# A gated hybrid decoder layer on eight cores: weights packed block by block, and the first projection of the head fed tile by tile

## The reference, cut to what matters

```
h    = rmsnorm(x, g_mix)
proj = h @ w_in                              # 1024 -> 3584: a | u | v | gate_a | gate_b
z    = gelu(proj[u, v])
v    = rmsnorm(z[v], g_v)                    # per row, over 512
s    = causal 128x128 mix of v inside each chunk of 128 rows (w_s, b_s)
pa   = (windowed means of a, windows 2,4,8,16, minus a) @ w_pool * s_pool
x    = x + (gate_a * (pa @ w_pool_out) + gate_b * ((u*s) @ w_gmlp_out)) @ w_out
h2   = rmsnorm(x, g_ffn)
x    = x + (silu(h2 @ w_gate) * (h2 @ w_up)) @ w_down
y    = rmsnorm(x, g_final)
```

## Time and profile before

| | us |
|---|---|
| median of 3 runs (872.39 to 930.36) | 873.85 |
| profiled execution, its own time | 876.13 |
| span of its slowest core, core 5 | 874.6 |
| spans of cores 0, 2, 3, 7 | 873.6, 867.3, 872.8, 873.3 |

### The profile page before, as it was taken

One profiled execution on the slowest core, in us unless ns is written; L12 is line 12 of the kernel. 1 busy time (PEld: TensorE's weight loads), 2 busy tenths in 40 slices (PEclk: granted clock), 3 DMA queues, 4 the chain that ended last, 5 costly groups with the idle time before them and its releaser, 6 DMA issues.

```text
span 874.6 us, 13055 instructions; the slowest of 8 cores (867.3 to 874.6 us)
## 1 busy us (share of the span) xinstructions
PE 824.1 (94%) x4584; PEld 437.0 (50%) x4584; DVE 370.3 (42%) x609; ACT 248.4 (28%) x452; POOL 142.3 (16%) x174
## 2 busy tenths in 40 slices
PE   0599999999999999999997999999999999999996
PEld 0346666655666666644443454444544444444442
DVE  1458644456322222244566593344722112114446
ACT  3654522224321121120146452222531111110012
POOL 2320011021201110000235211101120101000003
PEclk9989999999999999999998899999999999999998
DMA  8896346574966573544378942667587566356304
GB/s 205 191 139 87 73 56 86 75 103 69 113 81 81 65 93 43 84 70 75 54 209 233 110 56 28 80 85 98 68 99 95 65 81 85 50 84 88 57 16 177
DMA packets 102482, 81.05 MB, mean 93 GB/s; under 512 B 5324, under 2 KB 96964, under 8 KB 102403
## 3 DMA queue, kind: packets, MB, share of 16 engines
q0 software_dynamic: 94048, 58.10, 50.7%
q1 hardware_dynamic: 7390, 20.88, 7.5%
q10 hardware_dynamic: 981, 1.24, 0.7%
HBM read 129.76 MB, written 9.01 MB: 159 GB/s over the span
## 4 chain that ended last, share of the span: by engine, by line
PE 89%; DMA 5%; DVE 2%; issue 1%; ACT 1%; POOL 1%; SPq 1%; DVEq 0%; POOLq 0%; ACTq 0%
PE ps L346 87%; DMA xbuf<-xp 2%; DMA ring<-w_in 2%; PE ps L396 1%; DVE hb L384 1%; SPq L304 1%; POOL rs L364 0%; PE ps L647 0%; ACT hT L404 0%; PE ps L600 0%; DVE ps L653 0%; DVEq L926 0%; ACT junk L355 0%; DVE ovl L658 0%; DVE shr L538 0%
## 5 line engine op out<-in xcount | busy, mean ns | idle before, releaser
L346 PE MATMUL ps<-hT,ring 128*128 128x384 bf16 (+2 forms) x2720 | 489.9, 340 | 2.5 <-ACT hT L404 1.3
L346 PEld LDWEIGHTS ps<-hT,ring 128*128 128x128 bf16 x2720 | 266.2, 98 | 211.3 <-issue 11.4
L346 PE MATMUL ps<-ring,ovl 128*128 128x512 bf16 (+1 forms) x1020 | 224.3, 379 | 0.0
L748 DVE TENSOR_TENSOR ovl<-ftmp,ps 128x384 bf16<-128x384 f32 (+2 forms) x110 | 64.2, 585 | 241.0 <-PE ps L346 238.1
L346 PEld LDWEIGHTS ps<-ring,ovl 128*128 128x128 bf16 (+1 forms) x1020 | 97.8, 97 | 118.8 <-issue 4.3
L746 ACT ACTIVATE ftmp<-ps 128x384 f32<-128x384 f32 (+2 forms) x110 | 56.6, 515 | 240.5 <-PE ps L346 240.4
L355 ACT ACTIVATE junk<-xbuf 128x1024 bf16<-128x1024 f32 (+1 forms) x47 | 49.6, 1056 | 142.1 <-DVE xbuf L870 60.7
L364 POOL TENSOR_TENSOR rs<-ms,mhalf 128x1 f32<-128x1 f32 (+1 forms) x68 | 55.4, 817 | 181.5 <-DVE ms L360 181.5
L834 DVE TENSOR_TENSOR xbuf<-xbuf,ps 128x512 f32<-128x512 f32 (+1 forms) x68 | 46.7, 687 | 55.0 <-PE ps L346 54.1
L346 PE MATMUL ps<-ovl,ring 128*128 128x384 bf16 (+2 forms) x320 | 62.4, 338 | 0.0
L716 DVE TENSOR_TENSOR shr<-shr,ps 128x384 f32<-128x384 f32 (+2 forms) x40 | 23.4, 585 | 88.8 <-PE ps L346 80.0
(11 more groups left out here) (76 smaller groups left out, 380.2 us busy)
## 6 DMA issues: line engine op xcount, KB each, us to landing
ring<-w_gate POOLq DMA_DIRECT2D x22, 512.0 KB, 7.8
ring<-w_up POOLq DMA_DIRECT2D x22, 512.0 KB, 9.6
xbuf<-xp SPq DMA_DIRECT2D x16, 512.0 KB, 8.8
ring<-w_in POOLq DMA_DIRECT2D x16, 512.0 KB, 9.2
ring<-w_down POOLq DMA_DIRECT2D x8, 1024.0 KB, 9.4
ring<-w_in POOLq DMA_DIRECT2D x6, 1024.0 KB, 18.4
yp<-ybuf SPq DMA_DIRECT2D x11, 512.0 KB, 3.0
ring<-w_out POOLq DMA_DIRECT2D x4, 1024.0 KB, 13.2
```

The source lines that it names most:

```text
L346: ins = e.matmul(out=out, lhsT=lhs_fn(i), rhs=rhs_fn(i), start=(i == 0), stop=(i == n - 1))
L748: P.op('dve', lambda e: e.tensor_tensor(out=actT[:, f, c0:c0 + W], in0=ftmp[:, fi, :W], in1=PS[bU][:, :W], op=ALU.mult), reads=[('ftmp', f ...
```

## The change

Four things change; the second pass and all work behind D stay as they are.

1. The host packs all weights into one array `wpk`, block after block in the order of use, so that each of the 128 partitions finds its part of a block (up to 4096 elements) in one row. A block is one DMA.
2. In the head of the first pass C is the fifth stage of the pipeline (`head_stages`): the v matmuls of a tile stand right behind its transposes. The copy into `hT` goes to DVE for odd slots. Gelu of v is written to `vg`, a float32 buffer of eight tiles in a part of `ovl` that is not yet used.
3. The norm of v is taken out of C. The squares (`sq`, on ACT) follow the first nine pieces of B, and the mean, the power and the two multiplications (`v_tail`) come in two lots, after the fourth and the ninth piece. The multiplications are on POOL, one with the row scale and one with g_v. `ws_prep` follows the tenth piece.
4. ACT's queue carries only g_mix; the other constants follow the x tiles on SP's queue, each with a semaphore of its own. POOL issues the mixing matrices and block 1 after the powers of slots 0 to 2, then the rest. A first gelu on one column (after `memset` of `mhalf`) is put in front of ACT's work.

```diff
         def ring_issue(j):
             slot = j % NSLOT
-            for pi, (off, k, m, src) in enumerate(blocks[j]):
-                dst = slot_view(slot, off, k, m)
...
+            off, ne = blocks[j]
+            dst = ring[:, slot, 0:ne]
+            src = wpk[0:1, off:off + 128 * ne].rearrange("o (p e) -> (o p) e", p=128)
...
         def late_pool_consts():
+            cdma('pool', ws_nat[:, :, :], w_s.rearrange("g i j -> i g j"), 'ws_nat', own='c_wsnat')
+            ring_issue(1)
             cdma('pool', wpool_b[:, :, :], w_pool.rearrange("g c d -> c g d"), 'wpool', own='c_wpool')
-            cdma('pool', ws_nat[:, :, :], w_s.rearrange("g i j -> i g j"), 'ws_nat', own='c_wsnat')
             cdma('pool', bs_rep[:, :, :].rearrange("p g i -> p (g i)"), b_s[0:1, :].partition_broadcast(128),
                  'bs_rep', own='c_bsrep')
-            for j in range(1, NSLOT):
+            for j in range(2, NSLOT):
                 ring_issue(j)
...
-                pipeline([norm_stages(slot, R, col0, gmix_rep, 'gmix') for (slot, R, col0) in tts],
-                         [0, 1, 2, 3])
-                late_pool_consts()
-            if s == 0:
-                for (slot, R, col0) in tts:
-                    c_tile(slot, R, col0)
-                ws_prep()
+                kv = [newcol() for _ in range(9)]
...
+                def head_stages(slot, R, col0, wv=wv, cres_=cres_):
+                    ns = norm_stages(slot, R, col0, gmix_rep, 'gmix', copy_eng=('dve' if slot % 2 else 'act'))
+                    vs, vres = v_src(slot, R)
+
+                    def st_c():
+                        b = bank()
+                        P.op('pe', mm_group(PS[b][:R, :], lambda i: hT[:, i, col0:col0 + R],
+                                            lambda i: wv[:, i, :], 8),
+                             reads=cres_ + hT_res([slot]), writes=[('ps', b)])
+                        P.op('act', lambda e: e.activation(out=vs, in_=PS[b][:R, :], func=AF.Gelu_apprx_tanh),
+                             reads=[], writes=[vres, ('ps', b)])
...
+                def v_tail(lo, hi):
...
+                            P.op('pool', lambda e, slot=slot, k=k: e.tensor_scalar(
+                                out=vg[:, slot, :], in0=vg[:, slot, :], scalar1=rs[:, k:k + 1], scalar2=None,
+                                op0=ALU.mult),
+                                 reads=[('vg', slot), ('rs', k)], writes=[('vg', slot)])
+                            P.op('pool', lambda e, slot=slot: e.tensor_tensor(
+                                out=vtok[:, slot, :], in0=vg[:, slot, :], in1=gv_rep[:, :], op=ALU.mult),
+                                 reads=[('vg', slot), 'gv'], writes=[('vtok', slot)])
...
+                hsteps = [head_stages(slot, R, col0) for (slot, R, col0) in tts]
+                lags = [0, 0, 1, 2, 3]
+                for i_ in range(len(hsteps) + 3):
+                    for si_ in (0, 1, 2, 4, 3):
+                        t_ = i_ - lags[si_]
+                        if 0 <= t_ < len(hsteps):
+                            hsteps[t_][si_]()
+                    if i_ == 2:
+                        late_pool_consts()
+                v_rest = [(3, lambda: v_tail(0, 4)), (8, lambda: v_tail(4, 9)), (9, ws_prep)]
...
+                    it_ = g * len(nts) + ci
+                    if it_ < len(v_sq):
+                        v_sq[it_]()
+                    for (at_, fn_) in v_rest:
+                        if at_ == it_:
+                            fn_()
```

More of the change, by code:

```diff
@@ L25, with _wblocks @@
 ENGS = ('sp', 'pool', 'act', 'dve', 'pe')
+def _wblocks():
+    out = []
+    for cb in (2, 0, 1):
+        out.append([('w_in', 8, cb * 512, 512)])
+    for q in range(4):
+        out.append([('w_in', 8, 1536 + q * 256, 256), ('w_in', 8, 2560 + q * 256, 256)])
+        out.append([('w_po', 4, q * 256, 256), ('w_go', 4, q * 256, 256)])
+    for half in range(2):
+        out.append([('w_out', 8, half * 512, 512)])
+    for j in range(NF // 2):
+        out.append([('w_gate', 8, j * 256, 256), ('w_up', 8, j * 256, 256)])
+    for (f0, nf) in ((0, 6), (6, 8), (14, 8)):
+        for half in range(2):
+            out.append([('w_down%d' % f0, nf, half * 512, 512)])
+    return out
+WBLOCKS = _wblocks()
+WTOT = 128 * sum(k * m for blk in WBLOCKS for (_, k, _, m) in blk)
 class Prog:
@@ L240, in slot_view @@
             return ring[:, slot, off:off + k * m].rearrange("p (k m) -> p k m", k=k)
-        blocks = []
-        carry = {}
[L244 to L259, removed]
+        offs = []
+        o_ = 0
+        for blk in WBLOCKS:
+            e_ = sum(k * m for (_, k, _, m) in blk)
+            offs.append((o_, e_))
+            o_ += 128 * e_
+        blocks = offs * NSUP
+        carry = {}
         rstate = {'issued': 0, 'next': 0}
@@ L263, in ring_issue @@
             slot = j % NSLOT
-            for pi, (off, k, m, src) in enumerate(blocks[j]):
-                dst = slot_view(slot, off, k, m)
[L266 to L271, removed]
+            off, ne = blocks[j]
+            dst = ring[:, slot, 0:ne]
+            src = wpk[0:1, off:off + 128 * ne].rearrange("o (p e) -> (o p) e", p=128)
+            P.dma('pool',
+                  (lambda e, dst=dst, src=src: e.dma_start(out=dst, in_=src)),
+                  'w%d' % slot, reads=(), writes=[('ring', slot, 0), ('ring', slot, 1)])
             rstate['issued'] = j + 1
@@ L307, in build_nc @@
         cdma('act', gmix_rep[:, :], g_mix[0:1, :].partition_broadcast(128), 'gmix', own='c_gmix')
-        for slot in range(4):
+        for slot in range(9):
             xload(0, slot)
         cdma('pool', ident_b[:, :], c_ident[:, :], 'ident_b', own='c_idb')
[L311 to L315, removed]
@@ L329, in late_pool_consts @@
                 ring_issue(j)
[L330 to L335, removed]
+        cdma('sp', gv_rep[:, :], g_v[0:1, :].partition_broadcast(128), 'gv', own='c_gv')
+        cdma('sp', mask_f[:, :], c_mask[:, :], 'mask_f', own='c_mask')
+        cdma('sp', invcnt[:, :, :], c_invcnt.rearrange("p (g t) -> p g t", g=4), 'invcnt', own='c_inv')
@@ new lines, in build_nc @@
+        cdma('sp', sel[:, :, :, :], c_sel.rearrange("p (h g t) -> p h g t", h=2, g=4), 'sel', own='c_sel')
+        cdma('sp', stb[:, 0, :], st[0:120, :], 'stb', own='c_stb0')
+        cdma('sp', stb[:, 1, :], st[120:240, :], 'stb1', own='c_stb1')
+        cdma('sp', ident_f[:, :], c_ident[:, :], 'ident_f', own='c_idf')
+        cdma('sp', spT[:, :], s_pool.rearrange("o (g p) -> p (o g)", p=128), 'spT', True, own='c_sp')
+        cdma('sp', w00rep[:, :], w_s[:, 0, 0:1].rearrange("g o -> o g").partition_broadcast(128), 'w00', True, own='c_w00')
@@ L337, in build_nc @@
+        cdma('sp', b0rep[:, :], b_s.rearrange("o (g i) -> o g i", g=4)[:, :, 0].partition_broadcast(128), 'b0', True, own='c_b0')
+        cdma('sp', gffn_rep[:, :], g_ffn[0:1, :].partition_broadcast(128), 'gffn', own='c_gffn')
+        cdma('sp', gfin_rep[:, :], g_fin[0:1, :].partition_broadcast(128), 'gfin', own='c_gfin')
         P.dma('sp', lambda e: e.dma_start(out=nps[:, 0:14, :], in_=st3[:, 1:15, :]), 'omisc')
+        P.op('dve', lambda e: e.memset(mhalf[:, :], -0.5), writes=['mhalf'])
```

76 lines of the change are left out of this document (49 added, 27 removed).

## The result

| | before | changed kernel |
|---|---|---|
| runs shown ahead of the prediction, median | 873.85 | |
| all four runs of the comparison, median (range) | 899.91 (872.39 to 930.36) | 891.6 (891.49 to 892.37) |
| of these, the runs in the ratio, median | 873.12 (2 runs) | 891.6 (4 runs) |
| profiled execution | 876.13 | 892.37 |
| span of its slowest core, core 5 | 874.6 | 890.8 |

The ratio is 1.0214, with a 95% interval of 1.0189 to 1.0238: the change makes the kernel 2.1% slower, and whether by more than 2% stays open. (In some runs the cores of one die are granted a lower clock and take longer, 925.98 and 930.36 here; ratios and medians, from here on, are of the other runs.) The forecast was 874, its range 862 to 887: wrong, and outside the range.

What follows compares the result with a forecast made beforehand. PE was taken as the bound (busy 824.1 of 874.6 us), with gains only where it idles, mostly in the head. Terms -8.1 (earlier B) and +8.3 (norm on POOL) summed to +0.2: 874 us, range 862 to 887.

Steps and rivals of the forecast that it cites:

- start of B: End of the head: with C inside it, B starts at 50.8 us instead of 58.92, a term of -8.1 us.
- slot 8 later, from the start of B: D's first group waits for slot 8's v from POOL: 7.8 us late, plus 2.7 for waiting out DVE operations.
- given back in D: In D, 2.3 us of existing PE idle time come back as DVE's backlog clears during the wait.
- Norm of v in B: In B, 19 POOL operations at 1.08 us each make D's first group late: +5.5 us at least.
- POOL beside DVE: In B, POOL waits out running DVE operations; half of 5.4 us taken, 2.7, raising the cost to +8.3 us.
- The rival built on it: In B, DVE is locked out by POOL as well, slot 8 at S + 38: +13.5, 879 us; chance 0.17.
- S: The time at which B starts: 58.92 us before the change, forecast at 50.8.
- lose a little: In the head, x tiles lose a little to block 0's long packets and win back turns six constants took on q10.
- slow clock in the head: Rival: PE's clock stays at 1.2 GHz in the head, all tiles slow: 889 us (881 to 893); chance 0.15.
- The DMA rival: In the head, packets of blocks 1 to 3 delay x, C ends at 55: 878 us (874 to 883); chance 0.10.
- POOL cheap: Rival: POOL's operations in B cost 0.75 us each and the clock rises at once: 864 us; chance 0.15.
- slower by over 2%: Whole kernel above 891.3 us, the upper end of the slow clock with a dear POOL; chance 0.09.

Runs made afterwards that it cites:

- e9: Changed kernel with the first pass's long DVE pooling operations for g = 0 to 2 on 32 columns instead of 1024, that work left out; 886.89 us, ratio 1.0123.

## Why the prediction was wrong

The mechanism was the right one in the main: C gains in the head, D's first group waits for POOL, B waits for no block, nothing changes behind D. The sizes were off:

| term, us (core 5) | forecast | measured | off by |
|---|---|---|---|
| start of B | -8.1 | -3.9 (55.03 - 58.92) | 4.2 |
| slot 8 later, from the start of B | +10.5 (7.8 + 2.7) | +20.8 (42.81 - 22.05) | 10.3 |
| given back in D | -2.3 | -0.7 | 1.6 |
| sum | +0.2 | +16.2 | 16.0 |

**The step that failed is "Norm of v in B"**: the price of a wide POOL operation, taken as 1.08 us for each of 19. Alone they take 1.56 (one input and a scalar per row), 1.26 (two inputs) and 1.43 (the cast), 26.8 us for the 19 where I had 20.5. Of the 10.3 us this is 6.3. Another 2.6 are what stands between them: the second power (1.20), the wait for it (0.59) and small gaps come to 3.2 in e9's 30.0 us, and I had put 0.6 for the power and nothing for the rest. With the measured prices of the 19 alone the forecast's sum would have been +6.5 instead of +0.2, some 880 us and still inside the range; the other misses all went the same way. The bounds were wrong too: the lower end was a DVE price, and there was no upper end. The row of a one-column power (0.56) says nothing of what 512 columns cost on POOL, and the increment for them was DVE's. The Trainium skill's figures erred the same way: "GPSIMD Engine Reference", section 3.1, gives about 1.9 us a tile by the estimate in the prediction, and here a tile took 2.82.

**POOL beside DVE** was put at 2.7 and cost 3.6 (33.6 - 30.0): 0.9 of the 10.3. I let POOL wait and not DVE; the fences above show both. The Trainium skill ("SBUF — State Buffer", section "Who interferes with whom") says that the pair of ports is locked for a whole instruction and that the second to come is blocked, on either side. The trace agrees in part: 1.56 became 2.54 on POOL behind a DVE operation, and 1.24 became 2.25 on DVE behind an L512. Behind an L508 it became only 1.54, with both running, and no run here shows why. The rival built on it was right in kind; its price, 879, rested on the same 1.08, and it had D's first DVE step 8 to 10 us later, where it came 3.9 later (78.82 - 55.03 = 23.79, for 19.88). (The last 0.4 us are the start of the first lot, S + 9.0 for S + 8.8, and the step from the cast to PE.)

**Start of B.** From C's start to B's the forecast had 32.3 us (50.8 less 18.5), and it took 32.9: two slow tiles, then 3.3 to 3.6 apart, DVE's copy 0.69. (On the other seven cores one tile was slow, and the forecast had one and a half.) What was off is C's start, 22.17 for 18.5. Block 0 landed at 21.9 instead of 17 to 19, and x tile 2 at 19.44 instead of 16.92, because the long packets and the x packets share turns. The two queues from 12 to 20 us:

```profile
q0 software_dynamic: 125, 0.94, 74.2%
q1 hardware_dynamic: 139, 0.50, 25.2%
```

A packet of block 0 took 74.2% x 16 x 8 us / 125 = 760 ns, within the forecast's 0.8. What I had wrong is when they flow: from about 12 us instead of 10, and for almost 10 us instead of 8. From 10 to 12 us POOL's queue moved 127 packets with 0.12 MB in all, short ones still. And x did not "lose a little": q1 moved 0.50 MB in these 8 us, against 1.51 before.

**Given back.** D's idle time did go (17.43 busy of 17.54 us), but the stall had brought the clock down: the first matmuls behind it, 98.93, took 2.76 where the same group takes 1.46. From 98.11 to 101.81 PE needed 3.7 us for what took 1.9 before. A wait costs more than its own length.

**The rivals.** The slow clock in the head did not come: after two tiles no group of C's matmuls took over 1.89. The DMA rival did not either: no wait for x is left once C runs. POOL cheap is refuted by e9. I gave "slower by over 2%" to the slow clock together with a dear POOL, with a chance of 0.09; a dear POOL, with block 0 some 4 us late and a slow clock behind D's stall, came to 2.1% without a slow head.

## What to carry to other kernels

When an operation moves to an engine on which the trace shows nothing of its size, its price has no upper bound yet: take a multiple of the other engine's as the upper end, and ask from which price on the answer changes (here the forecast's own sum broke even at 1.08 us an operation, the very value taken). Work taken out of a stage has to go where its engine idles: the same norm costs 19 us more in B on POOL than in the head on DVE and ACT. A better DMA shape is worth what the wait behind it is worth: 2 us in one order of the program, 9 in another.

## What the runs showed of the hardware

- On POOL a multiplication of 128x512 float32 by a column took 1.56 us, and the product with another such tile 1.26: one input was dearer than two. With 16 partitions instead of 128 they took 1.55 and 1.26.
- POOL's multiplication by a column, where it came under a long DVE operation, ended 1.43 to 1.44 us behind it, and a long DVE operation that came under POOL's product of two tiles ended 1.08 to 1.09 behind that; the record of the second includes its wait (2.54 us for 1.56, 2.25 for 1.24). In e9 even DVE's mean on five columns took 1.28 us under such a product (66.91), where the one on four took 0.17 alone (60.57). Beside POOL's multiplication by a column a long DVE operation took 1.54 instead of 1.24, both running.
- TensorE kept the full speed for 22 us (33 to 55) of groups of eight matmuls with 0.7 to 1.3 us of idle time ahead of each, PE being busy for 71% of the stretch (15.63 us), and its grant fell to half (0.58 on average) in the stretch with waits of 3.6 to 6.5 us.
- 94,048 DMA packets became 9,984 for the same 58.1 MB, the queue's share of its engines fell from 50.7% to 36.6%, and no time came of it behind D (775.4 us from E's start to the end, for 775.5).
